# A hybrid retention and attention step: the bias table loaded by fewer, longer transfers

## The reference

```python
dr = row_idx - r[:, None] + (WIN_R - 1)          # 0..14
dc = np.clip(col_idx[:, None, :] - q_col[:, :, None], -(WIN_C - 1), WIN_C - 1) + (WIN_C - 1)   # 0..30
bias = rpb[:, dr[:, None, None, :, None], dc[None, :, :, None, :]].astype(jnp.float32)
bias = jnp.where(valid[None, None, :, :, None, :], bias, NEG_INF).reshape(h, rows, NA_NCB, NA_QB, wr * NA_KBW)
s_loc = jnp.einsum('bhrnqd,bhrnkd->bhrnqk', qg, kg).astype(jnp.float32) * scale + bias[None]
```

## Time and profile before

| | |
|---|---|
| median of 3 runs | 2003.96 us (2003.83 to 2005.5) |
| the profiled execution's own time | 2003.88 us |
| its span | 2002.1 us |
| mean granted TensorE clock | 0.945 of full speed |
| PE busy | 1825.5 us, 91% |
| DVE busy | 1160.4 us, 58% |
| ACT busy | 698.1 us, 35% |
| POOL busy | 272.1 us, 14% |
| DMA packets, of them under 512 B | 274605, 23029 |

### The profile page before, as it was taken

The page is one execution under the profiler, slowest core; times in us unless marked ns, Lnnn a source line. Parts: engine busy times, 40 slices in busy tenths (PEclk is TensorE's granted clock), DMA queues, the critical chain, the costliest instruction groups (busy, mean ns, idle before and its releaser), DMA issues.

```text
span 2002.1 us, 28780 instructions
## 1 busy us (share of the span) xinstructions
PE 1825.5 (91%) x11572; PEld 1647.5 (82%) x11572; DVE 1160.4 (58%) x2017; ACT 698.1 (35%) x1179; POOL 272.1 (14%) x262
## 2 busy tenths in 40 slices
PE   7899988379879999999988899999898999999998
PEld 3799853259779999999977886777787999999997
DVE  2777557364776676767574765565457653233345
ACT  2332234154442222313333454555444313132233
POOL 2200000142420000000242120011242000000012
PEclk9799989589889999999988799999998899999999
DMA  8244320102334545444331020000132442222232
GB/s 293 88 158 148 105 62 12 43 1 87 93 98 134 159 136 155 140 153 142 106 88 56 27 85 1 1 1 1 56 103 74 131 122 74 75 73 82 72 111 74
DMA packets 274605, 181.32 MB, mean 91 GB/s; under 512 B 23029, under 2 KB 249130, under 8 KB 274474
## 3 DMA queue, kind: packets, MB, share of 16 engines
q1 hardware_dynamic: 274474, 179.50, 29.3%
HBM read 175.92 MB, written 3.56 MB: 90 GB/s over the span
## 4 chain that ended last, share of the span: by engine, by line
PE 70%; DVE 11%; issue 5%; SPq 5%; ACT 5%; POOL 3%; DMA 1%; ACTq 0%; POOLq 0%; DVEq 0%
PE ps L630 18%; PE ps L632 18%; PE ps L631 18%; SPq L552 4%; PE ps L1099 4%; PE ps L1077 3%; DVE nt L1570 2%; ACT w_hi L414 2%; PE ps L1088 2%; PE ps L701 1%; DVE w_lo L423 1%; DVE nt L1568 1%; POOL rstd L2101 1%; DVE xT L1558 1%; PE ps L762 1%
## 5 line engine op out<-in xcount | busy, mean ns | idle before, releaser
L630 PE MATMUL ps<-hM_hi,w_lo 128*128 128x320 f32 x1120 | 361.9, 323 | 36.2 <-POOL hM_lo L2105 20.7
L414 ACT ACTIVATE w_hi<-stage 128x1024 fp32r<-128x1024 f32 (+2 forms) x230 | 239.2, 1040 | 405.3 <-PE ps L632 355.8
L423 DVE TENSOR_TENSOR w_lo<-stage,w_hi 128x1024 fp32r<-128x1024 f32 (+2 forms) x230 | 281.5, 1224 | 164.8 <-ACT w_hi L414 162.9
L630 PE MATMUL ps<-h_hi,w_lo 128*128 128x320 f32 x1152 | 359.8, 312 | 4.7 <-DVE w_lo L423 4.6
L632 PE MATMUL ps<-h_hi,w_hi 128*128 128x320 f32 x1152 | 357.2, 310 | 0.0
L631 PE MATMUL ps<-h_lo,w_hi 128*128 128x320 f32 x1152 | 357.1, 310 | 0.0
L631 PE MATMUL ps<-hM_lo,w_hi 128*128 128x320 f32 x1120 | 355.0, 317 | 0.0
L632 PE MATMUL ps<-hM_hi,w_hi 128*128 128x320 f32 x1120 | 354.6, 317 | 0.0
L630 PEld LDWEIGHTS ps<-hM_hi,w_lo 128*128 128x128 f32 x1120 | 216.7, 194 | 49.5 <-POOL hM_lo L2105 27.7
L2101 POOL TENSOR_TENSOR rstd<-rstd,sq 128x320 f32<-128x320 f32 x98 | 118.3, 1207 | 990.6 <-ACT sq L1148 987.5
L630 PEld LDWEIGHTS ps<-h_hi,w_lo 128*128 128x128 f32 x1152 | 217.0, 188 | 9.5 <-DVE w_lo L423 7.4
(11 more groups left out here) (287 smaller groups left out, 2928.3 us busy)
## 6 DMA issues: line engine op xcount, KB each, us to landing
stage<-in_w_mlp_in SPq DMA_DIRECT2D x76, 512.0 KB, 4.0
stage<-in_w_mlp_out SPq DMA_DIRECT2D x76, 512.0 KB, 4.2
slab_mlp<-in_w_ada SPq DMA_DIRECT2D x28, 1024.0 KB, 5.1
stage<-in_w_in_ac SPq DMA_DIRECT2D x28, 512.0 KB, 3.7
slab_ac<-in_w_ada SPq DMA_DIRECT2D x12, 1024.0 KB, 5.9
ada_a<-in_w_ada SPq DMA_DIRECT2D x8, 1024.0 KB, 8.6
stage<-in_w_out_ac SPq DMA_DIRECT2D x14, 512.0 KB, 4.1
stage<-in_w_out_c SPq DMA_DIRECT2D x14, 512.0 KB, 4.0
```

The source lines that it names most:

```text
L414: nc.scalar.activation(w_hi[:, n % 2, 0:width], stage[:, n % STAGE, 0:width], ACT.Copy)\
L423: nc.vector.tensor_tensor(w_lo[:, n % 2, 0:width], stage[:, n % STAGE, 0:width], w_hi[:, n % 2, 0:width].bitcast(F32), ALU.subtract).then_ ...
L630: mm(out, lo[:, k], xh, start=j == 0, stop=False)
```

## The change

A tensor `rpb_rows` of 8 heads x 8 rows x 248 elements is added in DRAM. One transfer fills it with turned copies of the table: for each head and `r`, the 8 table rows from row `7 - r` on, 248 contiguous elements, read from overlapping places. SyncE issues it behind the first two slabs. The tile `bias` gets a flat row of 272 elements for each head in place of 8 x 48, and 16 transfers fill it, one for each column `c`: 8 partitions, and for each 8 heads x 248 contiguous elements, written from element `c + 1` on. Before them SyncE waits for `rpb_rows`. The sums read `bias` through a view in which key row and key column have the steps 31 and 1, so that the rows of the view overlap; columns outside the table's row hold elements of neighbouring rows, and `mask` adds -1e30 to them.

`bias` and `mask` now lie together on memory that is free during retention. The load of `mask` stands behind the 16 transfers, ahead of the waits for `nkt` and `ret_out`. `nkt` moves onto the memory of `dist`, so ScalarE waits for all eight `d_exp` before it writes it. POOL clears only the 128 past keys' columns of `bm`, and waits for 16 transfers of bias in place of 128.

```diff
+BIAS_W = ROWS * RPB_C + 24
...
-        [bias] = lay(80, ("bias", [P, NH, ROWS, 48], F32))
-        mask, bm, pA, pTA = lay(
-            94, ("mask", [P, NB, NKEY], F32), ("bm", [P, 2, 2, NKEY + NP], F32), ("pA", [P, 6, 384], F32),
+        bias, mask = lay(80, ("bias", [P, NH, BIAS_W], F32), ("mask", [P, NB, NKEY], F32))
+        rpb_rows = nc.dram_tensor("rpb_rows", (NH, ROWS, ROWS * RPB_C), F32).ap()
+        bm, pA, pTA = lay(
+            98, ("bm", [P, 2, 2, NKEY + NP], F32), ("pA", [P, 6, 384], F32),
...
-        [nkt] = lay(92, ("nkt", [P, NH, HD], F32))
+        [nkt] = lay(134, ("nkt", [P, NH, HD], F32))
...
+            def table_rows():
+
+                rpb = i["na_rpb"][0]
+                at = rpb[:, ROWS - 1:ROWS, 0:1]
+                src = bass.AP(at.tensor, at.offset, [[RPB_R * RPB_C, NH], [-RPB_C, ROWS], [1, ROWS * RPB_C]])
+                sp.dma_start(rpb_rows[:], src).then_inc(rpb_in, 16)
...
             load_slab(1)
+            table_rows()
             sp.wait_ge(ada_done, ADA_START)
...
             sp.wait_ge(bias_zero, 1)
-            rpb = i["na_rpb"]
+            sp.wait_ge(rpb_in, 16)
             for c in range(BLK):
-                for r in range(ROWS):
-                    q = ROWS * c + r
-                    sp.dma_start(bias[q:q + 1, :, :, c + 1:c + 1 + RPB_C],
-                                 rpb[0:1, :, ROWS - 1 - r:2 * ROWS - 1 - r, :]).then_inc(na_bias_in, 16)
+                sp.dma_start(bias[ROWS * c:ROWS * (c + 1), :, c + 1:c + 1 + ROWS * RPB_C],
+                             rpb_rows[:].rearrange("h r x -> r h x")).then_inc(na_bias_in, 16)
+            sp.dma_start(mask[:], i["c_mask"]).then_inc(na_in, 16)
...
             sp.wait_ge(ret_out, PAIRS)
-            sp.dma_start(mask[:], i["c_mask"]).then_inc(na_in, 16)
...
                     act.wait_ge(nk_t, 1)
+                    act.wait_ge(d_exp, 2 * PAIRS)
...
-            nc.gpsimd.memset(bm[:], 0.0).then_inc(bias_zero, 1)
+            nc.gpsimd.memset(bm[:, :, :, NKEY:NKEY + NP], 0.0).then_inc(bias_zero, 1)
             pool.wait_ge(bias_zero, 2)
             pool.wait_ge(na_in, 16)
-            pool.wait_ge(na_bias_in, 16 * BLK * ROWS)
+            pool.wait_ge(na_bias_in, 16 * BLK)
...
+            def bias_window(h, u):
+
+
+                at = bias[:, h, u:u + 1]
+                return bass.AP(at.tensor, at.offset, [at.ap[0], [1, KW], [RPB_C, ROWS]])
...
-                        bias[:, 2 * m + e, :, u:u + KW].rearrange("p r c -> p c r"),
+                        bias_window(2 * m + e, u),
```

More of the change, by code:

```diff
@@ L273, in build @@
         ret_in, na_in, na_bias_in, mla_in = sem("ret_in"), sem("na_in"), sem("na_bias_in"), sem("mla_in")
+        rpb_in = sem("rpb_in")
         stored = sem("stored")
```

## The result

The changed kernel takes 1973.71 us, median of 4 runs (1971.74 to 1974.73), against 2004.73 us for the kernel before, measured beside it (median of 4, 2003.83 to 2006.16). The ratio is 0.9843, with a 95% interval from 0.9826 to 0.986: 31 us less. The forecast was 1975.5, between 1970.5 and 1981.0. The profiled execution took 1974.05 us; its span is 1972.2, 29.9 us shorter than before.

A forecast was written before the change was run, and what follows sets the result against it. The prediction took SyncE's 128 bias issues, which delay `mask` and POOL's sums, as the bound. Stall 29.1 us, minus 1.4 for the collision, plus 0.6 for row minima, gives 28.4 off 2003.88: 1975.5 us, range 1970.5 to 1981.

The forecast's parts named there:

- What bounds: SyncE's 128 bias issues delay `mask` and POOL's sums; the stall is worth 29.1 us, measured from the reciprocal's end.
- step 8: POOL's first four sums run beside VectorE's gate products and hold them until 350.4; 1.4 us reach the path.
- step 9: First four row minima no longer paced by POOL's sums: 2.24 us at 0.56 each instead of 2.88, gain 0.6.
- Step 1: The transfer writing turned copies adds one SyncE issue of 0.67 to 0.79 us behind the second slab, hidden: zero.
- Step 2: 16 bias issues on SyncE at 0.71 us each end at 295.7, or 297 if longer, where 375.6 stood.
- Steps 3 and 4: Bias landed by about 304, at worst 337; `mask` at 301, at worst 342; all hidden under retention until 343.5.
- slower rival: Bias transfers land late ahead of POOL's first sum; at 8.6 us each POOL starts at 426, giving 2049 us; 3%.
- Step 5: ScalarE's new wait for all decays before writing `nkt`: decays end at 324.4, `nkt` starts at 331.37, cost zero.
- Steps 6 and 7: POOL's `bm` memset shrinks to 0.46 us; 24 sums through the overlapping view stay at 0.875 us, bounds -3 and +3.
- The clock: TensorE's clock after the stall: at most 3.5 us gained, or 5.5 lost per extra attention-stage dip; neither taken.
- The first rival: TensorE's clock recovers after the shorter pause and no hold occurs: 1970.7 us, or 1967.7 with cheaper sums; 14%.

The follow-up runs named there:

- e1: Changed kernel with each of the 16 bias transfers split into 8, one per partition (128 transfers from the turned copies): 1991.24 us, ratio 0.9931 to the kernel before.
- e7: Changed kernel with 64 bias transfers of 2 partitions in place of 16 of 8: 1972.51 us, ratio 0.984 to the kernel before.
- e2: Changed kernel with the load of `mask` put back behind the wait for the end of retention: 1973.68 us, ratio 0.9847 to the kernel before.
- e3: Changed kernel with POOL's first sum held until the group norm's square root is there: 1974.85 us, ratio 0.9849 to the kernel before.
- e5: Changed kernel with nine more matmuls, results unread, in TensorE's two pauses before the group norm's spreads: 1973.93 us, ratio 0.9848 to the kernel before.
- e4: Changed kernel with its flat bias tile and early `mask`, but 128 transfers reading the input: 1995.88 us, ratio 0.996 to the kernel before.
- e6: Changed kernel with nine unread matmuls on TensorE and POOL's sums held until the square root: 1973.54 us, again 1972.45; ratios 0.9841 and 0.9847 to the kernel before.

## Why the prediction was right

- *What bounds*: right. The stall was worth what was left until the group norm's reciprocal. From `fin`, 28.5 us went; the forecast said 28.4. That they agree to 0.1 us is in part luck, because two errors cancel: the row minima start 28.3 us sooner, where 27.7 was forecast (step 8), and from there to the first product only 0.2 us are won, where 0.6 was forecast (step 9). Neither POOL's wait of 36.4 us nor the 91 us of issues was the measure.
- *Step 1*: right, one issue of 0.79 us at 45.4, hidden. `dist` is issued 0.3 us later than before and `fin` ends 0.35 later, but the second slab, issued ahead of the new transfer, is already 0.35 us later (43.19 against 42.84), so the new transfer costs nothing that shows.
- *Step 2*: an upper bound in effect. Free at 291.8, not 295.7: one issue every 0.44 us, not 0.71. No row of the kernel before could show that a transfer to a single partition is dear; e1 and e7 did.
- *Steps 3 and 4*: right in sign, all hidden. `mask` landed at 297.2, forecast 301. When the bias landed, no row shows; POOL's first sum at 344.51 was not released by a DMA, so it was there by then. The late landing of the slower rival has no trace; e7 hides its landings too.
- *Step 5*: right, no wait of ScalarE for the decays shows.
- *Steps 6 and 7*: the memset took 0.53 us for 0.46; the sums through the overlapping view have a median of 850 ns against 846, so the step of 31 costs what 48 did.
- *Step 8, the collision*: right in kind, mis-sized. 0.9 us reach the path, not 1.4. The forecast had VectorE wait out undisturbed sums and add its 3.03 us behind them. In fact the two series took turns and both slowed: the sums ended at 349.54, the products at 350.21, 5.7 us from the first start, where 6.3 us would be one series after the other. The Trainium skill's page "SBUF — State Buffer", section "Who interferes with whom", gave this term; e2 and e3 take it away by moving the sums. The Trainium skill's rule there, that the later of two blocks completely, fits the trace one instruction at a time, not one series at a time: each product took 1.47 us beside a sum against 0.82 without, and the median sum 1.43 us against 0.85.
- *Step 9*: the row minima followed each other every 0.48 us, not 0.56, but the step left out what comes behind them. The forecast let the first product start when they end; it also needs the spreads, which before had run during the stall. At half clock they ended at 357.04, the row minima at 356.25, and the product waited 0.73 us. This wait was in no term; e5, at full clock, has it no more.
- *The clock*: taken at nothing. From the first product to `out0` the first profile of the changed kernel is 2.0 us shorter than that of the kernel before, with a mean clock of 0.85 against 0.79. First the changed kernel, then the kernel before:

```profile
356.99:427.46 70.47, 54.06 (x449) 40.06 (x448) 47.07 (x175) 40.73 (x121) 24.59 (x25) 0.85 0.00 1
```

```profile
385.16:457.58 72.42, 56.85 (x448) 42.15 (x449) 46.82 (x177) 41.06 (x122) 25.48 (x26) 0.79 0.00 1
```

  No run ties these 2.0 us to the change: e4 has the stall and still takes 70.44 us, and one program took 69.8 and 72.1 us (e6 twice). Over the 14 profiles the stage goes from 69.6 us at a clock of 0.87 (e1) to 72.4 at 0.79 (before). Whether the clock makes it long, or waits in it lower the clock, stays open.

- *The first rival*, a clock that recovers because TensorE's pause falls from 30 us to 4: wrong. It was at 0.50 from 354 to 366, for 12 us, although TensorE was busy for 9.7 of them, and not at 1.0 from 358 on. e5, with the pauses ahead of 354 filled, kept 1.0 until then, so the pauses that are left, with light work between them, were enough to lose it. The rule of the Trainium skill's page "TensorE: Matmul & The Clock Gate", section "What's actually happening", that activity releases the clock, agrees with e5's 1.0 until 354, but taken by itself it does not foresee the 0.50 over the 12 us behind.

The forecast sum of 28.4 us lies beside 29.9 in span: 28.5 where it was worked out, 1.4 from the attention stage and scatter, of open cause, that only the range had covered.

## What to carry to other kernels

Size a stall by what ends next once it is gone, not by the wait in the list. When loads are moved out of the way, ask also what their consumer will now run beside: here loading `mask` early bought only a collision, and the stage had no use for the data that early. When a wait goes, ask what else the next instruction needs that the wait had hidden: here the spreads. A gain of one or two us ahead of a stage that varies by two us on its own needs more than end times to be judged; measure it by the distance between two events in the trace, in more than one profile.

## What the runs showed that was not expected

- Issuing a transfer on SyncE took 598 ns to one partition of `bias`, 272 ns to two and 306 ns to eight, for runs of 992 bytes (e1, e7, the changed kernel). Two partitions per transfer saved the whole stall (e7).
- Adjacent rows merge: laying the tile out flat cut the packets under 512 B from 23029 to 14845 with the old source (e4); the first product then came 41.67 - 34.29 = 7.4 us sooner than before, with as many transfers as before (their issues were 0.05 us cheaper each, and `mask` stood ahead of two stores).
- Four POOL sums beside four VectorE products, both reading two tiles in SBUF, took 5.03 and 5.65 us, against 3.27 and 3.03 apart. Side by side they needed 5.7 us in all, hardly less than the 6.3 of one after the other.
